# Sixteen state-space heads, taken two at a time on TensorE's column halves, in a two-layer decoder step

## What is computed

```python
acs = jnp.cumsum(ac, axis=2)                     # per head, within a chunk
causal = jnp.tril(jnp.ones((lc, lc), bool))
seg = jnp.exp(jnp.where(causal, acs[:, :, :, None] - acs[:, :, None, :], -jnp.inf))
cb = jnp.einsum('bctgn,bcsgn->bctsg', cc, bc)
y_diag = jnp.einsum('bctsg,bctsgr,bcsgrp->bctgrp', cb, seg, xc)
...
y_off = jnp.einsum('bclgn,bcgrpn,bclgr->bclgrp', cc, h_prev, jnp.exp(acs))
y = (y_diag + y_off).reshape(b, nc * lc, nh, hp)[:, :l]
```

## Time and profile before

| | us |
|---|---|
| median of 3 runs | 3794.18 (3792.93 to 3794.74) |
| the profiled execution | 3789.86 |
| its span | 3788.1 |
| PE busy in the span | 3376.0 (89%) |
| DVE busy | 1453.5 (38%) |
| ACT busy | 1007.6 (27%) |
| POOL busy | 377.6 (10%) |

### The profile page before, as it was taken

How to read it: one execution, slowest core, us unless ns; L and a number is a source line. 1 busy time by engine, 2 the same in 40 slices (tenths; PEclk the granted TensorE clock), 3 DMA queues, 4 the chain that set the end, 5 groups by cost and what they waited for, 6 DMA issues and landing times.

```text
span 3788.1 us, 54509 instructions
## 1 busy us (share of the span) xinstructions
PE 3376.0 (89%) x21318; PEld 3187.0 (84%) x21318; DVE 1453.5 (38%) x2188; ACT 1007.6 (27%) x1347; POOL 377.6 (10%) x271
## 2 busy tenths in 40 slices
PE   7985779799899999999799967697999899999997
PEld 6973459698899999999689956696989899999996
DVE  1565453615432222123403457856144422122126
ACT  2123441514231011011413323434232411111112
POOL 1664101000100000001000033010001000000001
PEclk9987999999999999999899989899999999999998
DMA  4673742325111111111121114322261111111112
GB/s 135 204 244 115 232 146 61 117 65 202 45 39 44 45 45 44 44 45 39 49 77 61 55 53 149 118 73 78 83 228 39 34 50 39 50 44 44 44 38 57
DMA packets 366737, 319.80 MB, mean 84 GB/s; under 512 B 19680, under 2 KB 308881, under 8 KB 366211
## 3 DMA queue, kind: packets, MB, share of 16 engines
q1 hardware_dynamic: 346527, 295.66, 25.0%
q10 hardware_dynamic: 19940, 21.96, 1.7%
q0 software_dynamic: 144, 0.52, 0.0%
HBM read 287.69 MB, written 30.74 MB: 84 GB/s over the span
## 4 chain that ended last, share of the span: by engine, by line
PE 74%; DVE 10%; issue 5%; DMA 4%; ACT 3%; POOL 2%; SPq 1%; DVEq 0%; ACTq 0%; POOLq 0%
PE ps L325 63%; PE ps L1692 2%; POOL kpage L1107 2%; DVE spl_w L310 1%; PE ps L1428 1%; PE ps L984 1%; PE ps L712 1%; DVE x L1473 1%; DVE acc L2318 1%; PE ps L1670 1%; PE ps L1034 1%; PE ps L1054 1%; ACT x L1487 1%; DMA vpage<-in_cache_fox_v 1%; DVE prob L999 1%
## 5 line engine op out<-in xcount | busy, mean ns | idle before, releaser
L325 PE MATMUL ps<-xs,spl_w 128*128 128x344 f32 x12456 | 1993.1, 322 | 44.2 <-DVE spl_w L310 25.7
L325 PEld LDWEIGHTS ps<-xs,spl_w 128*128 128x128 f32 x12456 | 1987.1, 190 | 47.1 <-DVE spl_w L310 27.6
L310 DVE TENSOR_TENSOR spl_w<-raw_w,spl_w 128x1024 fp32r<-128x1024 f32 x268 | 336.5, 1256 | 765.6 <-ACT spl_w L306 761.7
L325 PE MATMUL ps<-hs,spl_w 128*128 128x344 f32 x3168 | 513.5, 325 | 27.5 <-DVE hs L1911 27.5
L325 PEld LDWEIGHTS ps<-hs,spl_w 128*128 128x128 f32 x3168 | 512.0, 193 | 29.0 <-issue 29.0
L306 ACT CAST spl_w<-raw_w 128x1024 fp32r<-128x1024 f32 x268 | 279.4, 1042 | 394.8 <-PE ps L325 362.6
L1909 DVE TENSOR_TENSOR sum_x<-sq,ps 128x1032 f32<-128x1032 f32 x44 | 54.1, 1229 | 351.4 <-PE ps L325 351.4
L1412 POOL MEMSET sum_x<- 128x1032 f32 x6 | 5.8, 958 | 1683.9 <-DVE hs L1911 1468.8
L1893 ACT CAST hs<-sum_x 128x1032 f32 (+1 forms) x44 | 46.4, 1055 | 472.1 <-DVE sum_x L1909 472.1
L1107 POOL TENSOR_TENSOR kpage<-kpage,qb 128x1024 f32<-128x1024 f32 x64 | 153.3, 2420 | 94.6 <-DMA kpage<-in_cache_fox_k 94.4
L1378 DVE SCALAR_TENSOR_TENSOR x<-x,ps 128x1032 f32 (+1 forms) x48 | 58.9, 1228 | 269.3 <-PE ps L325 269.3
(11 more groups left out here) (370 smaller groups left out, 2921.6 us busy)
## 6 DMA issues: line engine op xcount, KB each, us to landing
kpage<-in_cache_fox_k SPq DMA_DIRECT2D x128, 256.0 KB, 3.3
vpage<-in_cache_fox_v SPq DMA_DIRECT2D x128, 256.0 KB, 2.9
raw_w<-in_w_gate SPq DMA_DIRECT2D x44, 512.0 KB, 3.7
raw_w<-in_w_up SPq DMA_DIRECT2D x44, 512.0 KB, 3.7
mkv<-in_cache_mem_k SPq DMA_DIRECT2D x16, 1024.0 KB, 8.6
raw_w<-in_w_down SPq DMA_DIRECT2D x32, 512.0 KB, 3.9
raw_w<-in_w_in_cd SPq DMA_DIRECT2D x28, 512.0 KB, 3.7
spill_d<-acc ACTq DMA_DIRECT2D x16, 516.0 KB, 2.7
```

What stands on the lines that cost most here:

```text
L310: dve.tensor_tensor(spl_w[:, s, 1], raw_w[:, s], spl_w[:, s, 0].bitcast(F32), ALU.subtract).then_inc(lo_ready, 1)
L325: mm = pe.matmul(ps[:, 3 * s + t, 0:width], spl_w[:, s, a, k], part[:, k, width * t:width * (t + 1)], start=(k == 0 and step == 0), stop=( ...
```

## The change

Heads are taken in pairs c = 0 to 7. POOL has no part in the stage any more: DVE multiplies exp(row) by C (`decayed`). The differences of odd heads go to ACT (`drop`): relu(own value - row), eight instructions of 128 columns, whose exponential then takes scale -1. Buffers become four each; the two new ones of each kind lie in memory that `spl_w` (split weights) uses outside this stage. ACT waits for the matmuls of head h - 4. SP's load waits for the even heads' differences (`head_diff` counts those alone) and for `head_exp`, which on ACT stands behind `drop`. PE waits for both heads of a pair and then alternates between them, so that matmuls that follow one another write different column halves. Products, chunks and results stay the same.

```diff
@@ -86,6 +86,10 @@
         band = sb("band", [P, 4, P])
         suf = sb("suf", [P, DECB * NPG * FH])
         raw_w = sb("raw_w", [P, 2, DC, P])
+        under_w = ExitStack()
+        beside_halves = sb("beside_halves", [P, 2, DC, P], F32, under_w)
+        head_too = sb("head_too", [P, 2, SEQ], F32, under_w)
+        under_w.close()
         spl_w = sb("spl_w", [P, 2, 2, DC, P], F32R)
         ident = sb("ident", [P, P])
         ones = sb("ones", [P, P])
@@ -2263,8 +2267,16 @@
 
 
 
-        m_buf = [acc[:, 0, 0:SEQ], acc[:, 1, 0:SEQ], hprev[:, NT - 1]]
-        ce_buf = [xbc[:, 8, 0:SEQ], xbc[:, 9, 0:SEQ]]
+        halves = beside_halves[:, :, DC // 2:DC].rearrange("p a k n -> p a (k n)")
+        m_buf = [acc[:, 0, 0:SEQ], acc[:, 1, 0:SEQ], hprev[:, NT - 1], head_too[:, 0]]
+        ce_buf = [xbc[:, 8, 0:SEQ], xbc[:, 9, 0:SEQ], head_too[:, 1], halves]
+
+        def in_halves(ap, like):
+            return ap.rearrange("p (a n) -> p a n", a=2) if like is halves else ap
+
+        def ce_block(h, i):
+            ce = ce_buf[h % 4]
+            return ce[:, i // 4, P * (i % 4):P * (i % 4 + 1)] if ce is halves else ce[:, P * i:P * (i + 1)]
 
         def tiled(ap):
             return ap.rearrange("p (i n) -> p i n", n=P)
@@ -2276,33 +2288,36 @@
                     sp.wait_ge(sem("last_stored"), 16)
                 if h >= 2:
                     sp.wait_ge(sem("head_exp"), h - 1)
-                    sp.wait_ge(sem("head_diff"), h - 1)
+                    sp.wait_ge(sem("head_diff"), h // 2)
                 sp.dma_start(work[:, h % 2], acs_d[h:h + 1, :].to_broadcast([P, SEQ])).then_inc(sem(f"row_loaded{h % 2}"), 16)
 
         def act_heads(act):
+            then = chain(act, "act")
+
             def e(h):
+                ce = ce_buf[h % 4]
                 act.wait_ge(sem(f"row_loaded{h % 2}"), 16 * (FH // 2 + h // 2 + 1))
-                if h >= 2:
-                    act.wait_ge(sem("head_products"), h - 1)
-                act.activation(ce_buf[h % 2], work[:, h % 2], ACT.Exp).then_inc(sem("head_exp"), 1)
-
-            def seg(h):
-                act.wait_ge(sem("head_diff"), h + 1)
-                act.activation(m_buf[h % 3], m_buf[h % 3], ACT.Exp).then_inc(sem("head_seg"), 1)
-            e(0)
-            e(1)
-            seg(0)
-            for h in range(SH):
-                if h + 1 < SH:
-                    seg(h + 1)
-                if h + 2 < SH:
-                    e(h + 2)
-
-        def pool_heads(pool):
-            for h in range(SH):
-                pool.wait_ge(sem("head_exp"), h + 1)
-                pool.tensor_tensor(ce_buf[h % 2], ce_buf[h % 2], xbc[:, 10 + h // (SH // SG), 0:SEQ],
-                                   ALU.mult).then_inc(sem("ce_ready"), 1)
+                if h >= 4:
+                    act.wait_ge(sem("head_products"), h - 3)
+                act.activation(ce, in_halves(work[:, h % 2], ce), ACT.Exp).then_inc(sem("head_exp"), 1)
+
+            def drop(h):
+                act.wait_ge(sem(f"row_loaded{h % 2}"), 16 * (FH // 2 + h // 2 + 1))
+                if h >= 4:
+                    act.wait_ge(sem("head_products"), h - 3)
+                for i in range(NT):
+                    b = slice(P * i, P * (i + 1))
+                    ins = act.activation(m_buf[h % 4][:, b], work[:, h % 2, b], ACT.Relu, bias=acs_n[:, i, h:h + 1], scale=-1.0)
+                then(ins)
+
+            for c in range(SH // 2):
+                h = 2 * c
+                e(h)
+                drop(h + 1)
+                e(h + 1)
+                act.wait_ge(sem("head_diff"), c + 1)
+                act.activation(m_buf[h % 4], m_buf[h % 4], ACT.Exp).then_inc(sem("head_seg"), 1)
+                act.activation(m_buf[(h + 1) % 4], m_buf[(h + 1) % 4], ACT.Exp, scale=-1.0).then_inc(sem("head_seg"), 1)
 
         def dve_heads(dve):
             dve.wait_ge(sem("state_products"), NT)
@@ -2311,13 +2326,22 @@
                 dve.wait_ge(sem(f"row_loaded{h % 2}"), 16 * (FH // 2 + h // 2 + 1))
                 if h == 2:
                     dve.wait_ge(pe_steps, step("lastT_ready"))
-                if h >= 3:
-                    dve.wait_ge(sem("head_products"), h - 2)
+                if h >= 4:
+                    dve.wait_ge(sem("head_products"), h - 3)
                 for i in range(NT):
                     b = slice(P * i, P * (i + 1))
-                    ins = dve.tensor_scalar(m_buf[h % 3][:, b], work[:, h % 2, b], acs_n[:, i, h:h + 1], 0.0,
+                    ins = dve.tensor_scalar(m_buf[h % 4][:, b], work[:, h % 2, b], acs_n[:, i, h:h + 1], 0.0,
                                             ALU.subtract, ALU.min)
                 ins.then_inc(sem("head_diff"), 1)
+
+            def decayed(h):
+                ce = ce_buf[h % 4]
+                dve.wait_ge(sem("head_exp"), h + 1)
+                dve.tensor_tensor(ce, ce, in_halves(xbc[:, 10 + h // (SH // SG), 0:SEQ], ce), ALU.mult).then_inc(sem("ce_ready"), 1)
+
+            def masked_in(h):
+                dve.wait_ge(sem("head_seg"), h + 1)
+                dve.tensor_tensor(tiled(m_buf[h % 4]), tiled(m_buf[h % 4]), cbT[:, h // (SH // SG)], ALU.mult).then_inc(sem("m_ready"), 1)
 
             def y(c):
                 dve.wait_ge(sem("head_products"), 2 * c + 2)
@@ -2326,33 +2350,38 @@
                                          in1=ps[:, b:b + 2, :].rearrange("p a n -> p (a n)"),
                                          op0=ALU.mult, op1=ALU.add).then_inc(sem("y_ready"), 1)
             diff(0)
-            for h in range(SH):
-                g = h // (SH // SG)
-                if h + 1 < SH:
-                    diff(h + 1)
-                dve.wait_ge(sem("head_seg"), h + 1)
-                dve.tensor_tensor(tiled(m_buf[h % 3]), tiled(m_buf[h % 3]), cbT[:, g], ALU.mult).then_inc(sem("m_ready"), 1)
-                if h % 2 and h > 1:
-                    y(h // 2 - 1)
+            for c in range(SH // 2):
+                decayed(2 * c)
+                decayed(2 * c + 1)
+                masked_in(2 * c)
+                if c + 1 < SH // 2:
+                    diff(2 * c + 2)
+                masked_in(2 * c + 1)
+                if c:
+                    y(c - 1)
             y(SH // 2 - 1)
 
         def pe_heads(pe):
-            for h in range(SH):
-                c = h // 2
-                rs = slice(SD * (h % 2), SD * (h % 2 + 1))
-                if h == 4:
+            for c in range(SH // 2):
+                if c == 2:
                     pe.wait_ge(act_steps, step("last_ready"))
-                if h % 2 == 0 and c >= 4:
+                if c >= 4:
                     pe.wait_ge(sem("y_ready"), c - 3)
-                pe.wait_ge(sem("ce_ready"), h + 1)
-                pe.wait_ge(sem("m_ready"), h + 1)
+                pe.wait_ge(sem("ce_ready"), 2 * c + 2)
+                pe.wait_ge(sem("m_ready"), 2 * c + 2)
+
+                def of(i, h):
+                    return ps[SD * (h % 2):SD * (h % 2 + 1), 2 * (c % 4) + i // 4, P * (i % 4):P * (i % 4 + 1)]
                 for i in range(NT):
-                    out = ps[rs, 2 * (c % 4) + i // 4, P * (i % 4):P * (i % 4 + 1)]
-                    cs = slice(SD * h, SD * (h + 1))
-                    mm = pe.matmul(out, xdt[:, i, cs], m_buf[h % 3][:, P * i:P * (i + 1)], start=True, stop=(i == 0))
+                    for h in (2 * c, 2 * c + 1):
+                        mm = pe.matmul(of(i, h), xdt[:, i, SD * h:SD * (h + 1)], m_buf[h % 4][:, P * i:P * (i + 1)],
+                                       start=True, stop=(i == 0))
                     if i:
-                        mm = pe.matmul(out, hprev[:, i - 1, cs], ce_buf[h % 2][:, P * i:P * (i + 1)], start=False, stop=True)
-                mm.then_inc(sem("head_products"), 1)
+                        for h in (2 * c, 2 * c + 1):
+                            mm = pe.matmul(of(i, h), hprev[:, i - 1, SD * h:SD * (h + 1)], ce_block(h, i),
+                                           start=False, stop=True)
+                            if i == NT - 1:
+                                mm.then_inc(sem("head_products"), 1)
 
 
         w_sp = xbc[:, 9, 0:GW].rearrange("p (g n) -> p g n", g=4)
@@ -2654,7 +2683,6 @@
             for L in range(DEPTH):
                 if L == 1:
                     pool_states(pool)
-                    pool_heads(pool)
                 pool_sums(pool, ("ab_out", "cd_out_y")[L], 3 * L)
                 pool_cross(pool, L)
                 pool_sums(pool, f"xo{L}", 3 * L + 1)
```

## The result

The changed kernel takes 3775.59 us (median of 5 runs, 3771.43 to 3779.61), the kernel before 3794.18 (5 runs, 3792.93 to 3796.90): ratio 0.9947 [0.9936, 0.9958]. The profiled execution took 3775.59 as well. Its page begins with

The account below looks back on a forecast made before the run. DVE, standing still beside POOL, bound the stage; afterwards a loop through PE. First pair at 2263.1 + 49.2 + 5.8 + 5.2 ends at 2323.3, not 2338.9: 15.6 us less, forecast 3779, range 3771 to 3788.

Parts of the forecast that it names:

- six periods: From the first pair's start on PE, six pair-to-pair distances of 8.2 us each, 49.2 us in all.
- POOL's standstill: DVE stands still while POOL multiplies in the stage: some 27 us lost to POOL's 41.7 us, gone when POOL leaves.
- ACT: Odd heads' differences on ACT: eight instructions take 2.44 us, at most 3.1; keeping them on DVE saves some 4 us less.
- The halves overlap: On PE, a pair's 60 records alternating column halves run 0.055 us apart, 3.5 us at full clock.
- The clock: PE falls to 1.2 GHz behind most gaps between pairs, adding 1.7 us to a pair's 3.5, giving 5.2.
- p: PE's time for one pair's matmuls, taken as 5.2 us; 3.5 at full clock, 6.8 at 1.2 GHz.
- DVE's floor: DVE's own work per pair: four products 4.56, one difference 1.57, one skip term 1.19, together 7.3 us.
- The new wait: DVE's next even difference waits for PE's previous pair, ahead of masking: period is PE's pair time + 3.0, 8.2 us.
- The full-clock rival: PE keeps full clock, 3.5 us per pair: 21 us saved, kernel 3773 us; chance 0.2.
- the odd row's loop: Odd row load waits for the previous odd row's exponential on ACT: 3.6 + 2.44 + 0.96 + some 0.5 = 7.5 us per pair.
- The take-turns rival: PE's column halves don't overlap, 6.8 to 8.5 us per pair: 10 us slower, kernel 3804 us; chance 0.05.
- The next stage: Its loads start when the last heads' matmuls end, so each microsecond saved before 2338.9 is one of the kernel.

Follow-up runs that it names:

- the masking first: Changed kernel with DVE masking the odd head before taking the next even head's difference: 3777.96 us, ratio 0.9950, stage 77.48 us.
- a third buffer: Changed kernel with a third buffer for even heads' differences, so a difference waits for a head two pairs back: 3774.81 us, ratio 0.9955, stage 76.70 us.
- the second profile of the changed kernel: Changed kernel measured again with nothing changed, on the chip of two other runs: 3779.48 us, ratio 0.9962, stage 77.81 us.
- the run with the fillers: Changed kernel with ten unused identity products on PE between pairs: 3774.44 us, ratio 0.9947, stage 75.27 us.

## Why the prediction was right

I forecast 3779, and it is 3775.59, within the range; the repeat on another chip gave 3779.48 and a smaller gain, so that the hit is this close is in part luck. By its own steps, with distances within the stage:

| step | predicted, us | measured, us |
|---|---|---|
| first load issued to first pair on PE | 21.0 | 21.1 |
| six periods | 6 x 8.2 = 49.2 | 48.9 |
| last period | 5.8 | 5.7 |
| last pair's matmuls | 5.2 | 3.5 |
| the stage | 81.2 | 79.25 |

- **POOL's standstill.** Right: eight differences take 1.58 from start to the next instruction, beside nothing, as in the earlier trace rows. That it was the main term is shown by putting POOL back and by taking it out of the kernel before. That DVE stands still for as long as POOL works is too wide, as three places in the kernel before show:

```profile
2301.39 1.21 DVE L2334 TENSOR_TENSOR hprev<-hprev,work 128x1024 f32<-128x1024 f32 x1
2301.45 3.36 POOL L2304 TENSOR_TENSOR xbc<-xbc 128x1024 f32<-128x1024 f32 x1 [1.04 <-ACT xbc L2287]
...
2307.32 1.27 DVE L2325 SCALAR_TENSOR_TENSOR xbc<-xbc,dskip,ps 128x1024 f32<-128x1024 f32 x1
2307.44 2.37 POOL L2304 TENSOR_TENSOR xbc<-xbc 128x1024 f32<-128x1024 f32 x1 [2.63 <-ACT xbc L2287]
...
2331.83 2.36 POOL L2304 TENSOR_TENSOR xbc<-xbc 128x1024 f32<-128x1024 f32 x1 [2.45 <-ACT xbc L2287]
2332.73 2.54 DVE L2334 TENSOR_TENSOR acc<-acc,work 128x1024 f32<-128x1024 f32 x1 [0.76 <-ACT acc L2291]
```

A masking that had begun kept its 1.21, and POOL's product took 3.36 in place of 2.36; a masking that met a product under way took 2.54. The skip term, one of whose operands lies in the accumulator `ps`, kept its 1.27 beside POOL, and POOL its 2.37. So a difference or a masking that meets POOL's product stands still, a masking that began first holds POOL up instead, and the skip term and POOL leave each other alone.
- **ACT.** Right: the eight instructions take 2.43, at the lower bound and the value taken from the earlier trace rows. With these differences on DVE the stage took 5.2 us more, and I had given 4, as 0.7 for each of six periods. The six periods took 4.7 more; the last one, which then holds a difference too, took 1.6 more, and the first pair started 1.1 sooner. The rule of the Trainium skill (ScalarE: Activation LUTs, Rules for kernel authors) that wants relu on VectorE agrees with the trace for the instructions alone (387 ns against 280), and not for this stage.
- **The halves overlap.** Right: 3.49 for 60 records at full clock, against 3.5 predicted from the attention, and 6.34 with the same records in turn. The records show how, here in the fourth pair of the changed kernel (`hprev` serves the even head, `head_too` the odd one):

```profile
2295.62 0.27 PE L2377 MATMUL ps<-hprev,xdt 128*64 128x128 f32 x1
2295.65 0.27 PE L2377 MATMUL ps<-head_too,xdt 128*64 128x128 f32 x1
2295.73 0.27 PE L2377 MATMUL ps<-hprev,xdt 128*64 128x128 f32 x1
```

Each half keeps the 0.11 from record to record that one head had alone, and the other half's record lies in between; each record has a weight load of its own (60 of both in each window). So the statement of the Trainium skill (TensorE: Matmul & The Clock Gate, Part 3: Packing small matmuls) that weight loads overlap only with another row group does not hold for these column halves.
- **The clock.** Right in kind: it fell behind some gaps and not behind others. The term was mis-sized: p was 5.2 for every pair, and measured 5.56, 6.36, 5.12, 3.49, 3.50, 5.15, 5.02 and 3.49, on the mean 4.7. For the six periods this comes out even by luck, because DVE's floor catches the short pairs. For the last pair it doesn't, and its 1.7 us are most of the 2 by which the stage is better than forecast.
- **The new wait.** Right: where p was over 5 and a difference followed, the gap was 3.03 each time, and the term p + 3.0 holds to a few hundredths. The runs with the masking first and with a third buffer both remove the wait, but shorten the stage by only 1.8 and 2.6 us (0.3 and 1.1 against the second profile of the changed kernel, which is within the scatter), as the next loops stand close behind.
- **The full-clock rival.** Its p was right and its loop was not. I let the odd row's loop of 7.5 bind; the masking-first run measures that loop at the load plus 3.6, 7.2 with a load of 3.6, since handing over four times costs some 0.2 (3.6 less 2.44 and 0.96) and not 0.5. So DVE's floor of 7.3 ends last, as the run with the fillers shows. With full clock throughout I gave 21 us saved; that run's stage is 21.6 shorter, its first pair still below full clock.
- **The take-turns rival.** Not the case, and its sum would have been wrong for heads in turn: p is as priced (6.34 against 6.8, 8.12 against 8.5), but the loop p + 3.0 takes the whole pair, where the difference waits only for the even head, and another loop, over two pairs, sets a mean period of 8.5. What a rival with alternating heads and halves in turn would have given was not tried.
- **The next stage** moved with the end of the heads, as the earlier trace rows had it: PE's wait for the gv load ended at 2332.69, 5.2 after the loads' issue, and 5.0 before.

## What to carry to other kernels

Before giving an engine's idle time any value, look at what its work does to its neighbours: here POOL's 41.7 us of products cost DVE 26 (52.7 less 26.5), and DVE doing that work itself came out cheaper than sharing it. Write a stage with several engines as loops, each a sum of rows and the longest of them the period; when one is cut the next one shows how much of the cut is kept, and here three lay within one microsecond. The cut that saved most was none of these but the start of the stage, where one load waited for a store only because of a shared buffer.

## What was not expected

- With POOL back and the other parts of the change kept, the gain was 2.0 us of 17.6, less than with POOL's removal alone (9.5): the events that release the difference and POOL's product are then the same one, so every difference but the first meets a product.
- PE's clock fell or held behind gaps of the same 3.03 us: 0.53 in the pair that began at 2277.95 and 1.00 in the one at 2295.49. What tells them apart no view shows; it stays open. With unused matmuls in the gap, which leave 1.38 us of it, every pair from the second on had 1.00, at p = 3.50.
- Programs that are the same up to this stage reached it up to 13 us apart from one profile to the next, nearly all of it from before 560 us; a change inside one stage is seen better in that stage's length than in the time of the kernel.
